# Two modulations in one accumulation, gates spread through DRAM, finer first waits, and 17 extra products

## What is computed

```python
def adaln(cvec, w, b):
    m = jax.nn.silu(cvec) @ w + b
    return m.reshape(cvec.shape[0], N_MOD, D_MODEL)

def modulate(h, m, i):
    return h * (1.0 + m[:, i + 1][:, None, :]) + m[:, i][:, None, :]
...
        m = adaln(c_ctx[None, :], w_ada[l], b_ada[l])
        h = modulate(rmsnorm(x_ctx, norm1_g[l]), m, 0)
        o, kc, vc, hf, hb = mixer_context(h, *mix_w)
        x_ctx = x_ctx + m[:, 2][:, None, :] * o
        h = modulate(rmsnorm(x_ctx, norm2_g[l]), m, 3)
        x_ctx = x_ctx + m[:, 5][:, None, :] * moe(h, *moe_w)
```

## Time and profile before

| | |
|---|---|
| median of 3 runs | 900.0 us (899.17 to 901.62) |
| the profiled execution | 896.39 us |
| its span, first to last instruction | 894.5 us |
| PE busy | 855.6 us, 96% |
| DVE, ACT, POOL busy | 491.5, 242.8, 87.0 us |
| mean granted TensorE clock | 0.991 |

### The profile page before, as it was taken

One profiled execution on the slowest core, in us unless ns is written; L12 is line 12 of the kernel. 1 busy time (PEld: TensorE's weight loads), 2 busy tenths in 40 slices (PEclk: granted clock), 3 DMA queues, 4 the chain that ended last, 5 costly groups with the idle time before them and its releaser, 6 DMA issues.

```text
span 894.5 us, 13521 instructions
## 1 busy us (share of the span) xinstructions
PE 855.6 (96%) x4887; PEld 501.8 (56%) x4887; DVE 491.5 (55%) x1016; ACT 242.8 (27%) x398; POOL 87.0 (10%) x202
## 2 busy tenths in 40 slices
PE   3799999999999999999999999999999999999993
PEld 2387875899999874434444444444444444444441
DVE  1663384486667456245646464646464646464575
ACT  3537643444423241221111111121112121112122
POOL 8410000000001060000000000000000000000000
PEclk9999999999999999999999999999999999999997
DMA  9974877622225377499999999999999999999931
GB/s 353 343 288 163 299 290 255 141 95 95 95 95 170 149 296 317 190 413 409 416 420 403 410 420 419 404 416 419 420 421 414 420 421 421 417 420 404 421 126 70
DMA packets 76596, 280.82 MB, mean 314 GB/s; under 512 B 14340, under 2 KB 30784, under 8 KB 51584
## 3 DMA queue, kind: packets, MB, share of 16 engines
q1 hardware_dynamic: 61488, 260.06, 73.3%
q0 software_dynamic: 6352, 15.52, 4.6%
q10 hardware_dynamic: 8704, 4.54, 2.0%
HBM read 279.82 MB, written 5.51 MB: 319 GB/s over the span
## 4 chain that ended last, share of the span: by engine, by line
PE 90%; DMA 5%; DVE 3%; issue 1%; ACT 0%; ACTq 0%; DVEq 0%
PE bank L1488 26%; PE bank L1507 13%; PE bank L1516 11%; PE bank L1090 8%; PE bank L1092 7%; PE bank L1091 7%; PE bank L1476 4%; DMA chunk_raw<-in_w_ada_dram 3%; PE bank L1360 2%; DMA b_t<-in_b_ada_dram 2%; PE bank L1600 2%; PE bank L1118 1%; PE bank L1170 1%; PE bank L1404 1%; PE bank L1203 1%; PE bank L1277 1%
## 5 line engine op out<-in xcount | busy, mean ns | idle before, releaser
L1488 PE MATMUL bank<-gu,x_t 128*32 128x512 f32 (+2 forms) x1408 | 240.6, 594 | 0.0
L1488 PEld LDWEIGHTS bank<-gu,x_t 128*32 128x32 f32 (+2 forms) x1408 | 75.6, 124 | 147.4 <-issue 146.7
L2125 DVE TENSOR_TENSOR ffn_acc<-ffn_acc,bank 128x512 f32<-128x512 f32 x192 | 120.4, 683 | 7.8 <-PE bank L1516 6.6
L1507 PE MATMUL bank<-dn,a_t 128*32 128x512 f32 (+2 forms) x704 | 123.9, 596 | 0.0
L1050 ACT ACTIVATE silu_sb<-bank 128x256 f32<-128x256 f32 x34 | 13.0, 384 | 320.8 <-PE bank L1488 320.8
L2067 DVE TENSOR_TENSOR act_sb<-silu_sb,bank 128x256 f32<-128x256 f32 x34 | 14.3, 421 | 149.9 <-ACT silu_sb L1050 149.9
L1090 PE MATMUL bank<-h_hi,chunk_lo 128*128 128x384 f32 x240 | 84.2, 351 | 0.0
L2117 DVE SCALAR_TENSOR_TENSOR y_lo<-bank,slot_gate,y_hi 128x512 fp32r<-128x512 f32 x68 | 50.9, 748 | 55.8 <-ACT y_hi L1040 55.5
L1092 PE MATMUL bank<-h_hi,chunk_hi 128*128 128x384 f32 x240 | 80.6, 336 | 0.0
L1091 PE MATMUL bank<-h_lo,chunk_hi 128*128 128x384 f32 x240 | 80.4, 335 | 0.0
L747 POOL DMA_INDIRECT xg<-h_dram,slot_tok x34 | 33.9, 997 | 456.5 <-DVE slot_tok L1941 456.2
(11 more groups left out here) (359 smaller groups left out, 1043.2 us busy)
## 6 DMA issues: line engine op xcount, KB each, us to landing
gu<-in_w_gate_e_dram SPq DMA_DIRECT2D x64, 1024.0 KB, 10.3
gu<-in_w_up_e_dram SPq DMA_DIRECT2D x64, 1024.0 KB, 13.6
dn<-in_w_down_e_dram SPq DMA_DIRECT2D x64, 1024.0 KB, 14.2
chunk_raw<-in_w_ada_dram SPq DMA_DIRECT2D x24, 1024.0 KB, 8.5
chunk_raw<-in_w_in_dram SPq DMA_DIRECT2D x18, 1024.0 KB, 5.5
chunk_raw<-in_w_out_dram SPq DMA_DIRECT2D x4, 1024.0 KB, 5.1
chunk_raw<-in_w_pa_dram SPq DMA_DIRECT2D x2, 1024.0 KB, 5.0
chunk_raw<-in_w_pb_dram SPq DMA_DIRECT2D x2, 1024.0 KB, 5.0
```

The lines of the kernel that those rows point to most:

```text
L1488: mm = pe.matmul(bank[2 + u % 2][at_x, :].rearrange("p (g n) -> p g n", g=2), x_t[:, cols], wide[:, :, k, :], start=(k == 0), stop=(k == K ...
L1507: mm = pe.matmul(outs[half][at_x, :], a_t[:, cols], dn[slot_of(x, first)][:, wc], start=(k == 0), stop=(k == 1))
L2125: dve.tensor_tensor(ffn_acc[t][:, cols], ffn_acc[t][:, cols], out[:, :], ALU.add).then_inc(S["place_out"], 1)
```

## The change

- Modulations are made two at a time. A chunk of `w_ada` now has one k and all 1024 columns of two modulations (0 and 1, 3 and 4, 2 and 5), and eight chunks are accumulated into one bank: 6 for the first two pairs, 7 for the gates. The columns of 0, 1, 3 and 4 are read by PE with a step of eight elements, so that the four transposes that follow give the order in which the modulated x wants them; there is no sum over quarters. The later chunks are used by `later(j)`, two a call, at the places of the old `modulate`.
- The gates get their bias in rows (`bias_rows`, loaded by POOL), are stored to DRAM (`gate_dram`) and loaded back to all partitions by POOL's queue (`spread_rows`). `spread`, `pick`, `fold`, `m_late` and ACT's `spread_copy` go.
- The first projection waits for each part of `h_t` by itself, from the second on; `h_ctx` and `h_made` count every part.
- `keep_busy(n)`: n products of `ident` with 512 columns of `xhat` into bank 7, which nobody reads. Two stand behind each of the first seven chunks' products, and three behind the first transposes: 17.

```diff
 MODS = (0, 1, 3, 4, 2, 5)
-NADA = 4 * len(MODS)
+NMOD = len(MODS) // 2
+NADA = KD * NMOD
...
+                if kind == "ada":
+                    m, k = MODS[2 * (i // KD):2 * (i // KD) + 2], i % KD
+                    sp.dma_start(dst[:, :].rearrange("p (m n) -> p m n", m=2),
+                                 w_ada[0].rearrange("(p k) (m n) -> p k m n", k=KD, n=D)[:, k, m[0]:m[1] + 1:m[1] - m[0], :]).then_inc(loaded, 16)
...
+            pool.wait_ge(S["ada_row"], NMOD)
+            for c in range(2):
+                pool.dma_start(gate_dram[c:c + 1, :].rearrange("a (q n) -> (a q) n", q=NQ), gate_rows[c:P:QW, :]).then_inc(S["gate_stored"], 16)
+            pool.wait_ge(S["gate_stored"], 32)
+            pool.wait_ge(S["gates_mm"], 16)
+            def spread_rows(dst, n, loaded):
+                pool.dma_start(dst[:, :, :], gate_dram[:, D * n:D * n + D].unsqueeze(0).to_broadcast([P, 2, D])).then_inc(loaded, 16)
+            spread_rows(gate_mix, 0, S["mix_loaded"])
             pool.wait_ge(S["w_mm"], NPROJ)
...
+            spread_rows(gate_ffn, 1, S["ffn_gate_loaded"])
...
+            def modulate(i):
+                n, (m, k) = number[("ada", i)], divmod(i, KD)
+                pe.wait_ge(chunk_loaded[slot[n]], arrival[n])
+                if i == 0:
+                    pe.wait_ge(S["cond_silu"], 1)
+                elif i == KD:
+                    pe.wait_ge(S["mod_copied"], 2)
+                for q in range(NQ):
+                    cols = chunk_raw[slot[n]][:, q // 2 * D:q // 2 * D + D]
+                    if m < 2:
+                        mm = pe.matmul(bank[6][q * QW:(q + 1) * QW, :].rearrange("p (k n) -> p k n", k=4), cond_t[:, k, :],
+                                       cols.rearrange("p (n k) -> p k n", k=KD)[:, 4 * (q % 2):4 * (q % 2) + 4, :],
+                                       start=(k == 0), stop=(k == KD - 1))
+                    else:
+                        mm = pe.matmul(bank[7][q * QW:(q + 1) * QW, :], cond_t[:, k, :],
+                                       cols[:, 512 * (q % 2):512 * (q % 2) + 512], start=(k == 0), stop=(k == KD - 1))
+                mm.then_inc(S["ada_mm"], 1)
+            def turn_rows(m):
+                pe.wait_ge(S["ada_row"], m + 1)
+                for j in range(4):
+                    mm = pe.transpose(bank[6][:, j * P:(j + 1) * P], m_row[m][:, j * P:(j + 1) * P], ident[:, :])
                 mm.then_inc(S["m_spread"], 1)
+            def keep_busy(n):
+                for t in range(n):
+                    pe.matmul(bank[7][:, :], ident[:, :], xhat[:, t, 0:512], start=True, stop=True)
+            for i in range(KD):
+                modulate(i)
+                if i < KD - 1:
+                    keep_busy(2)
+            turn_rows(0)
+            keep_busy(3)
             pe.wait_ge(S["vec_loaded"], 7 * 16)
...
-                        if n == 0 and k % 4 == 0:
-                            pe.wait_ge(S["h_ctx"], k // 4 + 1)
-                            pe.wait_ge(S["h_made"], k // 4 + 1)
+                        if n == 0:
+                            pe.wait_ge(S["h_ctx"], k + 1)
+                            pe.wait_ge(S["h_made"], max(k + 1, 2))
...
-            for n in range(4):
-                if n >= 2:
-                    pe.wait_ge(S["bc_evac"], n - 1)
-                spread(n, bank[4 + n % 2], m_row[0])
-            pe.wait_ge(S["ada_row"], NADA // 2)
+            later(7)
+            pe.wait_ge(S["ada_row"], NMOD)
...
-                    if first and u == SPREAD_TURN:
+                    if first and u == 0:
                         pe.wait_ge(S["shd_evac"], 2 * TT)
-                        pe.wait_ge(S["late_row"], 1)
...
-                        for n in range(4):
-                            spread(n, spread_bank(n), m_late)
...
+            def modulations(m):
+                dve.wait_ge(S["m_spread"], m + 1)
+                by_half = bank[6][:, :].rearrange("p (j a h c) -> p a h j c", j=4, a=2, h=2)
+                for a in range(2):
+                    i = MODS[2 * m + a]
+                    dve.tensor_tensor(mod_t[:, i, :, :].rearrange("p (h j) c -> p h j c", h=2), by_half[:, a, :, :, 0:2],
+                                      b_t[:, i, :].rearrange("p (h j) -> p h j", h=2).unsqueeze(3).to_broadcast([P, 2, 4, 2]),
+                                      ALU.add).then_inc(S["mod_copied"], 1)
+            def gates_in_rows():
+                dve.wait_ge(S["ada_mm"], NADA)
+                dve.wait_ge(S["row_biased"], 64)
+                go(dve.tensor_tensor(gate_rows[:, :], bank[7][:, :], bias_rows[:, :], ALU.add))
+                dve.tensor_scalar(gate_rows[0:HALF, :], gate_rows[0:HALF, :], 0.5, None, ALU.mult).then_inc(S["ada_row"], 1)
```

More of the change, by code:

```diff
@@ L1101, in _ @@
                 mm.then_inc(S["xt1"], 1)
-            def modulate(a, h):
-                for r in range(2):
-                    n = number[("ada", 4 * a + 2 * h + r)]
-                    pe.wait_ge(chunk_loaded[slot[n]], arrival[n])
-                    if n == 0:
-                        pe.wait_ge(S["cond_silu"], 1)
-                    if r == 0 and a:
-                        if a < 5:
-                            pe.wait_ge(S["mod_copied"], a)
-                        else:
-                            pe.wait_ge(S["ada_row"], 2 * a - 1 + h)
-                        if a == 2:
-                            pe.wait_ge(S["vec_copied"], 1)
-                    for q in range(NQ):
-                        mm = pe.matmul(bank[6 + h][q * QW:(q + 1) * QW, :], cond_t[:, r * NQ + q, :],
-                                       chunk_raw[slot[n]][:, q * 512:q * 512 + 512], start=(r == 0), stop=(r == 1))
-                    mm.then_inc(S["ada_mm"], 1)
@@ L1122, in turn_rows @@
-            def turn_rows(a):
-                pe.wait_ge(S["ada_row"], 2 * a + 2)
-                for k in range(KD):
-                    mm = pe.transpose(bank[6 + k // 4][:, (k % 4) * P:(k % 4 + 1) * P], m_row[a % 2][:, k:D:KD], ident[:, :])
-                mm.then_inc(S["m_spread"], 1)
-            def spread(n, out, row):
-                pe.matmul(out[:, :], pick[:, n // 2, :], row[:, 512 * (n % 2):512 * (n % 2) + 512],
-                          start=True, stop=True).then_inc(S["bc_mm"], 1)
@@ L1132, in modulate_first @@
-            def modulate_first(a):
-                for c in range(4):
-                    n = number[("ada", 4 * a + c)]
-                    pe.wait_ge(chunk_loaded[slot[n]], arrival[n])
-                    if n == 0:
-                        pe.wait_ge(S["cond_silu"], 1)
-                    if c == 0 and a:
-                        pe.wait_ge(S["mod_copied"], a)
-                    for h in range(2):
-                        for j in range(2):
-                            q = 2 * ((c + h) % 2) + j
-                            at_w = j * D + 512 * h
-                            mm = pe.matmul(bank[6 + h][q * QW:(q + 1) * QW, :], cond_t[:, 2 * c + j, :],
-                                           chunk_raw[slot[n]][:, at_w:at_w + 512], start=(c < 2), stop=(c >= 2))
-                    mm.then_inc(S["ada_mm"], 1)
@@ L1665, in _ @@
             dve.wait_ge(S["cond_loaded"], 80)
-            for a in range(2):
-                dve.wait_ge(S["ada_mm"], 4 * a + 4)
-                row(a, 0)
-                mod_sum(a)
+            dve.wait_ge(S["ada_mm"], KD)
+            dve.tensor_copy(m_row[0][:, :], bank[6][:, :]).then_inc(S["ada_row"], 1)
+            modulations(0)
             dve.wait_ge(S["mod_copied"], 2)
@@ L1753, in _ @@
             dve.engine_nop().then_inc(S["ob_ready"], 1)
-            row(5, 0)
             low(10)
-            row(5, 1)
+            gates_in_rows()
             low(11)
```

140 lines of the change are left out of this document (40 added, 100 removed).

## The result

The changed kernel takes 921.4 us (median of 4 runs, 920.85 to 921.6); the kernel before took 899.6 in the same comparison. The ratio is 1.0239, with a 95% interval of 1.0223 to 1.0256. The forecast was 904.0, range 896 to 912: the side was right, the size was not. The profiled execution took 921.6 us.

What follows compares the result with a forecast made beforehand. PE was taken to bound the kernel, busy 855.6 of 894.5 us. The terms 5.5 + 7.6 - 0.7 - 1.65 + 1.7 - 1.3 - 0.8 - 2.4 - 4.0 made +4.0 us, so 900.0 becomes 904.0, range 896 to 912.

Steps and rivals of the forecast that it cites:

- `b_t` +5.5: Front: `b_t` lands later because queues alternate packet by packet and pieces become 8 KB; first product 5.5 us later, at 23.5.
- Rival B: Front: `b_t` lands as before, if pieces stay 4 KB or queues do not alternate so; 896.8 us, chance 0.17.
- the prediction's 1.6 us: Front: by the skill's rule of 9 to 17 descriptors a turn, larger weights delay `b_t` by 1.6 us at most.
- A chunk's four products at 0.91: Chunks of `w_ada`: four products side by side take 0.91 us, before and after; nothing charged for the stepped read.
- Rival C: Chunk products: the stepped read costs; a doubling is +14.6 us, 918.6; chance of a cost over 5 us 0.14.
- The 17 products +7.6: Front: 14 unread products at 0.86 us among eight chunks stretch that chain from 11.7 to 19.3 us, +7.6.
- -0.7 to the first projection: From last chunk to first projection: fewer transposes save time, other savings lie hidden under three unread products; -0.7 us.
- The clock -1.65 and +1.7: First projection at full clock, -1.65 us; PE idling before the first product costs one clock fall, +1.7 us.
- the cold start: Front: PE idles 7.4 us before the first product, charged one clock fall of +1.7 us, bounds 0 and 2.5.
- Middle -2.1: Later chunks: one set of four transposes replaces two of eight, -1.3 us; shorter waits for chunks, -0.8 us.
- -2.4 before attention: Before attention: four `spread` products go, PE waits for `gates_in_rows` instead, scores begin at 154.15; -2.4 us.
- -4.0 in the experts: Experts: four `spread` products and a short wait go, so `gate_up(1)` starts at 379.2 instead of 383.20; -4.0 us.

Runs made afterwards that it cites:

- experiment 2: The kernel before, with only its first eight chunks read with the step of eight elements and the transposes after them packed: 904.8 us, ratio 1.0059.
- experiment 10: The kernel before, but `cond_t` waits for its own two small loads and not for `b_t`: 901.3 us, ratio 1.0043.

## Why the prediction was right on the side and wrong on the size

- **`b_t` +5.5:** measured +5.6, and by the mechanism that it names (packets one for one, 8 KB pieces joined). Rival B fell. The Trainium skill, DMA: Bandwidth & Descriptors, section Queues, rings and completion order, gives a turn of about 9 to 17 descriptors. The delay alone does not speak against it: the prediction's 1.6 us let only ACT's queue pass so many in a turn, and if both did, `b_t` would be as late as one for one. The short stretch does: 27 against 27 within half a microsecond, in which each of the 16 engines passes only one or two of the weights' pieces.
- **A chunk's four products at 0.91, "before and after":** this step failed. They took 1.86 to 1.95. In the front that is 7.6 us over the forecast, in the middle 8 chunks for another 7.6 (3.79 against 1.90 for a pair). Rival C was this case; it had +14.6, measured +15.2. I had taken nothing for it, because the stepped weight load looked as quick as the packed one. That was the wrong row, and misread. The 0.12 us were the pace of eight transposes, in which a longer load is hidden: the kernel before has its stepped loads at L1125 at a median of 189 ns and the packed ones of the same size at L1476 at 140 (experiment 2 has both in one line). And a weight load is another operation than a moving operand's read. The step of 32 bytes was plain in the diff, and a chance of 0.14 was too low where no row showed the operation. The cachelines section of the Trainium skill (Advanced Engine Details and Errata) spoke against it, and the trace agrees: 1.95 against 0.91 us.
- **The 17 products +7.6:** the price of 0.86 was the row's. They took 0.96, and 1.06 with the first pair at half clock: 14.8 instead of 12.0 us for 14. The chain that they stand in came to 29.7 instead of 19.3 us: 7.6 from the step, 1.4 from the products' price, 0.7 from the clock and 0.7 from the joints (a stepped chunk takes 1.95 us between wide products and 1.86 in a row of its kind).
- **-0.7 to the first projection:** measured -0.7; the last three products hide DVE's work.
- **The clock -1.65 and +1.7:** measured -1.0 and about +0.7, the latter inside the 29.7. The first projection did run at full clock (granted 1.00), but takes 10.76 us and not 10.2: pricing it by the mean clock was too generous.
- **Middle -2.1:** the transposes (0.44 instead of 2 x 0.88) and the waits for chunks (0.7 instead of 1.3) came as forecast; with the step it is +5.6.
- **-2.4 before attention, -4.0 in the experts:** measured -2.4 and -3.9. No wait of PE for the copies by way of DRAM is in the trace.
- **Not in the forecast:** the gather behind the weights. In the profiled pair its stretch is +3.9. In the medians it seems to be less: probably some executions of the kernel before have the wait too, as that of experiment 10 has; its only trace, of an execution 3.2 us under the median of this comparison, has not. My sum was made against that execution and then moved to the median, which hid this term.

In medians: 921.4 - 904.0 = 17.4 us. The front is 10.4 over its forecast (less 1.7 charged apart for the cold start), the middle 7.6, the clock in the projection 0.6: 16.9. The other 0.5 is less than the spread of the runs. So the size was missed by one term, a chunk's four products, for 15.2 of the 17.4 us. Rival C's 918.6 had this term nearly right (14.6 for 15.2); the other 2.2 us to the measured 921.4 are the products' price, the joints, the clock and what is left open.

## What to carry to other kernels

Look at the step of the moving operand before anything else is priced: with float32 here, 8 bytes cost 5% and 16 or more doubled the product, while a set of eight transposes of 128 columns with the step on the stationary side takes 0.88 us in all, 0.11 each, the pace of packed ones. Read such a price from the record of the very operation, and not from the pace of a row in which it may lie hidden. When a layout can put the step on either side, put it on the small one. A small load that gates the first work waits in turns, not in bytes: when the big transfers' pieces grow, it comes later; give what gates the start its own semaphore. And when two queues are released by the same event, write down which is to go first with a wait; being issued first was not enough here when it was by 0.27 us.

## What the runs showed of the hardware

- A moving operand's step: 1.91, 2.00, 3.78 and 3.84 us for two products at 1, 2, 4 and 8 elements, and in the same ratio for four narrow products side by side (1.74, 1.83, 3.68, 3.67). I had expected that a lone product would have rate to spare.
- The time of a stepped chunk hardly depends on PE's clock: 2.04 us at a granted 0.50, 1.95 at 1.00. Packed chunks took 1.83 and 0.91.
- A weight load of a transpose, 128x128, took 0.14 us packed and 0.19 with a step of 8 elements; the transposes went at 0.11 each in both cases.
- Two queues fed by SP and ACT took turns piece by piece: 1468 to 1327 packets with 4 KB pieces on SP's side, 954 to 958 with 8 KB ones, 27 to 27 in half a microsecond.
- A 128-wide product between groups of narrow ones took 0.96 us; in a row of its own kind 0.86.
- A gather issued from 0.24 us behind to 0.27 us ahead of the first of two 1 MB loads of weights landed after 8.9 to 9.1 us; issued 1.2 us or more ahead of them, after 4.2 to 4.6.
- The granted clock was 0.50, that is 1.2 GHz, from 20.0 to 26.8 us, with PE idle before 23.6, and from 381.8 to 388.6, with PE idle from 380.5 to 383.2. In the packed kernel with the early `cond_t`, filling gaps of about a microsecond between chunks kept it at 2.4 GHz (1.00 instead of 0.74 in that stretch).
